# Causal mask of a second attention: added by VectorE in PSUM instead of by TensorE products, with one filling tile moved

## Chip, cores and metric

One core of one Trainium2 chip. The metric is the device time of one execution, in microseconds; three runs of the kernel before are given, and one more execution was profiled.

## The reference, cut to what matters

Two transformer blocks over 512 tokens of width 1024, in float32. The change lies in the attention of the second block, the "forgetting" attention with 16 heads of 64:

```python
def fox_attention(h, w_in, b_f, w_out):
    proj = h @ w_in                       # q, k, v of 16 heads, and 16 forget logits
    log_f = jax.nn.log_sigmoid(f_logit)
    c = lax.cumsum(log_f, axis=1).transpose(0, 2, 1)
    ...
        s = jnp.einsum('bhqd,bhkd->bhqk', qb, k, preferred_element_type=jnp.float32)
        s = s + cb[..., :, None] - c[..., None, :]
        s = jnp.where(k_pos[None, :] <= q_pos[:, None], s, NEG_INF)
        pr = jax.nn.softmax(s, axis=-1)
        return jnp.einsum('bhqk,bhkd->bhqd', pr.astype(v.dtype), v)
    ...
    return o @ w_out
```

All large products are computed in a split form: each operand is a high and a low part, and a product is three matmuls (high x high, high x low, low x high).

## The kernel before, in words

Every engine has its instructions in one order written out by hand, and semaphores tie them together. The weights come in "units" of 128 x 1024 (512 KB). SyncE loads a unit (L410), ScalarE makes its high part `w_hi` (L1856, helper `highs`), GpSimd its low part `w_lo` (L472), and TensorE multiplies it. Three buffers of each form a ring, so ScalarE's conversion of unit u + 3 waits until TensorE has finished unit u.

The second attention works in eight pairs of heads, p = 0 to 7. Its projections are 24 units, three per pair (q, k, v in that order). Eight "tiles" make up a unit; a tile is three matmuls of 128 x 512 (L519 to L521). Tiles are not done in a stage of their own: they fill the time in which the attention's chain would hold TensorE up. The list `FOX_FILL` (L179) says how many tiles stand behind each of the twelve places of a pair; `FOX_AHEAD` = 24 tiles are done before. The helper `fill` issues them, and `fox_made(p, i)` counts how many are done after place i. VectorE and ScalarE use the same count in `fox_evict`: when a unit is complete they scale it out of its bank (L1145), make its high part (L1845; q and k only) and its low part (L1622 or L1151), and ScalarE converts the weights of the unit three further on. For the last pair (p = 7) there are no tiles left and the first seven places hold steps of the output projection (`fill_out`).

TensorE's order in a pair (L1017 to L1030) is:

```python
scores(0); more(0)
scores(1); v_turn(); more(1)
scores(2); more(2)
scores(3); more(3)
turn(0, 0); turn(0, 1); more(4); pv(0, 0); turn(0, 2); more(5); pv(0, 1); turn(0, 3); more(6); pv(0, 2)
turn(1, 0); pv(0, 3); turn(1, 1); more(7)
pv(1, 0); turn(1, 2); more(8); pv(1, 1); turn(1, 3); more(9); pv(1, 2); more(10); pv(1, 3); more(11)
```

- `scores(qi)`, qi = 0 to 3, takes the query block qi of both heads against the first (qi + 1) * 128 keys, into PSUM banks 2 and 3. It waits until both exponentials of the step before are done (`A2["exps"]`). Four terms (L982) use 64 rows of the array for each head, the fourth adds the forget sums `c_head`; then one 128 x 128 product per head (L984), identity times the mask tile `causal_r` (0 on and below the diagonal, -1e30 above), adds the causal mask to the diagonal block and raises `A2["scores"]`.
- VectorE, `mx(qi)`: for each head `peak` (L1320 to L1322) waits for `A2["scores"]` and takes the negated row maximum. Between the steps stand `nrm(qi)` (reciprocal L1328, scaling L1331), the evictions, `out_low` and the low part of v, in this order: `mx(0)`, eviction and `out_low` of the pair before, `nrm(0)`, `mx(1)`, eviction, `nrm(1)`, `fv_lo`, `mx(2)`, eviction, `nrm(2)`, `mx(3)`, eviction, `nrm(3)`.
- ScalarE: two exponentials with row sums (L1992) per step, the high part of v (`fv_hi`), the next pair's `c_head` (L2260), and the conversions of the units.
- `turn(hd, kb)` transposes probabilities (L1000), ScalarE and VectorE split them into `fpt_hi` and `fpt_lo` (L1845, L1151), and `pv(hd, kb)` multiplies them with v (L1007 to L1009), waiting for `fpt_lo`.

Of the kernel before, what the change touches and what calls it, by code (L numbers as in the profile page):

```python
# [17 lines left out]
P = 128  # L18
# [23 lines left out]
F32 = mybir.dt.float32  # L42
F32R = mybir.dt.float32r
ALU = mybir.AluOpType
# [131 lines left out]


FOX_AHEAD = 24
FOX_FILL = [(2, 2, 3, 4, 2, 1, 1, 2, 1, 1, 1, 1)] * 6 + [(2, 2, 2, 3, 2, 1, 1, 1, 1, 1, 1, 1)]  # L179


def fox_made(p, i):

    return 3 * DC + FOX_AHEAD + sum(map(sum, FOX_FILL[:p])) + sum(FOX_FILL[p][:i + 1])

# [23 lines left out]
def build(nc, x_in, p_in, weights, vectors, last_gain, out):  # L209
# [4 lines left out]
    with ExitStack() as ctx:  # L214
# [7 lines left out]
        def sem(name):  # L222
            return ctx.enter_context(nc.semaphore(name))
# [17 lines left out]
        ident_r = sb("ident_r", [P, P], F32R)  # L241
        causal_r = sb("causal_r", [P, P], F32R)
# [95 lines left out]
        ps = ctx.enter_context(nc.psum_tensor("ps", [P, 8, S], F32))  # L338
# [23 lines left out]
        def stage_sems(stage, *names):  # L362
            return {n: sem(f"{stage}_{n}") for n in names}
# [8 lines left out]
        att_names = ("scores", "peak", "exps", "inv", "probs", "turned", "hi", "lo", "pv", "ohi", "olo")  # L372
        A1 = stage_sems("nsa", *att_names, "q", "qhi")
        s_cs = stage_sems("cmp_att", "scores", "sub", "exp", "stat", "probs")
        A2 = stage_sems("fox", *att_names, "qk", "qkhi", "vturned", "vhi", "vlo", "crow")
        s_fg = stage_sems("forget", "dve", "act")
        s_ffn = stage_sems("ffn", "tap", "conv", "t2", "gelu", "h", "hhi", "t")
        s_mlp = stage_sems("mlp", "t", "r", "s", "hi")
# [137 lines left out]
        def _(pe):  # L516
# [174 lines left out]
            for half in range(2):  # L691
                cols = slice(2 * P + half * P, 2 * P + (half + 1) * P)
                mm = three(ps[0:2 * NC1, 5, 0:P], hid_hi[:, 1, half, :], w_hi[:, uu % RING, cols], hid_lo[:, 1, half, :],
                           w_lo[:, uu % RING, cols], half == 0, half == 1)
# [45 lines left out]
            def fill(n):  # L740

                for at in range(made[0], made[0] + n):
                    part(u0 + at // DC, at % DC, at % DC + 1)
                made[0] += n
# [55 lines left out]
            for j in range(9):  # L800
                b = j - 1
# [31 lines left out]
            for tb in range(QB):  # L833
                mm = pe.matmul(ps[:, 3, tb:tb + 1], T[:, 1, tb * P:(tb + 1) * P], mean_ch[:, 0:1], start=True, stop=True)
# [3 lines left out]
            for tb in range(QB):  # L838
                mm = pe.matmul(ps[:, 3, tb * P:(tb + 1) * P], rms_c[:, 1, tb:tb + 1].to_broadcast([P, P]), ident[:], start=True, stop=True)
# [120 lines left out]
            def fox_here(k):  # L960
                pe.wait_ge(A2["olo"], CREDIT + 2 * k + 2)

# [6 lines left out]
            def fox_pair(p):  # L969

                par = p % 2
                q, k = (fq_hi[:, par, :], fq_lo[:, par, :]), (fk_hi[:, par, :], fk_lo[:, par, :])

                def scores(qi):

                    e, n = 8 * p + 2 * qi, (qi + 1) * P
                    pe.wait_ge(A2["exps"], e + 2)
                    qs = slice(qi * P, n)
                    for t, (a, b) in enumerate(((q[0][:, qs], k[0]), (q[0][:, qs], k[1]), (q[1][:, qs], k[0]), (ones_r, c_head))):
                        for hd in range(2):  # L980
                            rows = slice(hd * HD, (hd + 1) * HD)
                            pe.matmul(ps[:, 2 + hd, 0:n], a[rows, :], b[rows, 0:n], start=t == 0, stop=False)  # L982
                    for hd in range(2):
                        pe.matmul(ps[:, 2 + hd, qs], ident_r[:], causal_r[:], start=False, stop=True).then_inc(A2["scores"], 1)  # L984

                def v_turn():
                    pe.wait_ge(bank_free, u0 + 3 * p + 3)
                    pe.wait_ge(A2["lo"], CREDIT + 8 * p)
                    for tb in range(QB):
                        mm = pe.transpose(ps[:, 4, tb * P:(tb + 1) * P], fv[:, 0, tb * P:(tb + 1) * P], ident[:])  # L990
                    mm.then_inc(A2["vturned"], 1)

                def turn(hd, kb):
                    e = 8 * p + 4 * hd + kb
                    pe.wait_ge(A2["lo"], e + 1)
                    if kb == 0:
                        pe.wait_ge(A2["probs"], CREDIT + 8 * p + 7 + hd)
                    for qi in range(kb, QB):
                        off = P_OFF[qi] + kb * P
                        mm = pe.transpose(ps[:, 4 + kb % 2, qi * P:(qi + 1) * P], fprob[:, hd, off:off + P], ident[:])  # L1000
                    mm.then_inc(A2["turned"], 1)

                def pv(hd, kb):
                    pe.wait_ge(A2["lo"], 8 * p + 4 * hd + kb + 1 + CREDIT)
                    o = ps[:, 6 + hd, kb * P:S]
                    ph, pl = (t[:, kb % 2, kb * P:S] for t in (fpt_hi, fpt_lo))
                    pe.matmul(o, fv_hi[:, kb, :], ph, start=kb == 0, stop=False)  # L1007
                    pe.matmul(o, fv_hi[:, kb, :], pl, start=False, stop=False)
                    pe.matmul(o, fv_lo[:, kb, :], ph, start=False, stop=kb == QB - 1).then_inc(A2["pv"], 1)  # L1009

                def more(i):
                    if p < 7:
                        fill(FOX_FILL[p][i])
                    elif i < DC - 1:
                        fill_out(i)

                pe.wait_ge(bank_free, u0 + 3 * p + 2)  # L1017
                pe.wait_ge(A2["crow"], p + 1)
# [4 lines that stand above are left out]
                pe.wait_ge(A2["vlo"], p + 1)  # L1023
                pe.wait_ge(A2["olo"], p * 2 + 1)
                turn(0, 0); turn(0, 1); more(4); pv(0, 0); turn(0, 2); more(5); pv(0, 1); turn(0, 3); more(6); pv(0, 2)
                turn(1, 0); pv(0, 3); turn(1, 1); more(7)
                pe.wait_ge(A2["olo"], p * 2 + 2)
                if p == 0:
                    pe.wait_ge(bank_free, u0 + 6)
                pv(1, 0); turn(1, 2); more(8); pv(1, 1); turn(1, 3); more(9); pv(1, 2); more(10); pv(1, 3); more(11)  # L1030
# [75 lines left out]
            for h in range(2):  # L1106
                for j in range(4):
# [3 lines left out]
                    for kk, tb in (cells if h == 0 else sorted(cells, key=lambda c: c[1])):  # L1111
# [9 lines left out]
                        mm = three(ps[:, BANK[acc], :], xh, wh, xl, wl, k == 0, k == DC - 1)  # L1121
# [7 lines left out]
            for n in range(DC):  # L1129
# [5 lines left out]
                for m in range(4):  # L1135
                    mm = pe.transpose(ps[:, TURN_BANKS[n], m * P:(m + 1) * P], X[:, 4 * h + m, tb * P:(tb + 1) * P], ident[:])
# [4 lines left out]
        def _(dve):  # L1141
# [176 lines left out]
            scaled(U["gates"], T[:, 0:1, :])  # L1318

            def peak(A, e, par, st, qi, b):  # L1320
                dve.wait_ge(A["scores"], e + 1)
                dve.tensor_reduce(st[:, 0, par, qi:qi + 1], ps[:, b, 0:(qi + 1) * P], AX.X, ALU.max, negate=True).then_inc(A["peak"], 1)  # L1322

            def normalise(A, e, i, par, st, pr, qi, gate=None):
# [103 lines left out]
            for j in range(9):  # L1428
                p, br, b = j // 2, j % 2, j - 1
# [217 lines left out]
            for first in (32, 96):  # L1647
                rows = slice(first, first + 32)
# [18 lines left out]
            def fox_pair(p):  # L1667
                e0 = 8 * p

                def mx(qi):  # L1670
                    for hd in range(2):
                        peak(A2, e0 + 2 * qi + hd, hd, fstat, qi, 2 + hd)

                def nrm(qi):
                    for hd in range(2):
                        e = e0 + 2 * qi + hd
                        normalise(A2, e, e, hd, fstat, fprob[:, hd, :], qi)

                def lo(hd, kb):
                    split_turned(A2, e0 + 4 * hd + kb, kb % 2, (fpt_hi, fpt_lo), kb)  # L1680

                def out_low(p, hd):
                    rows = slice(hd * HD, (hd + 1) * HD)
                    dve.wait_ge(A2["ohi"], 2 * p + hd + 1)
                    low(fo_lo[rows, p:p + 1, :], ps[rows, 6 + hd:7 + hd, :], fo_hi[rows, p:p + 1, :], A2["olo"])

                def evict(i):
                    fox_evict(p, i)

                mx(0)  # L1690
                if p:
                    fox_evict(p - 1, 11)
                    out_low(p - 1, 1)
                nrm(0)
                mx(1); evict(0); nrm(1)
                dve.wait_ge(A2["vhi"], p + 1)
                low(fv_lo[:], ps[:, 4, :].rearrange("p (a b) -> p a b", b=P), fv_hi[:], A2["vlo"])
                mx(2); evict(1); nrm(2)
                mx(3); evict(2); nrm(3)
                evict(3)  # L1700
                lo(0, 0); lo(0, 1); evict(4); lo(0, 2); evict(5); lo(0, 3); evict(6); lo(1, 0); out_low(p, 0); lo(1, 1); evict(7)
                lo(1, 2); evict(8); lo(1, 3); evict(9); evict(10)
                if p == 7:
                    out_low(7, 1)
# [79 lines left out]
            for m in range(DC):  # L1784
                b, c, x = (bank(u0 + 3 * m + j) for j in range(3))
# [716 lines left out]
```

## Time and profile before

| what | us |
|---|---|
| three runs | 2181.45, 2186.0, 2184.88 |
| median | 2184.88 |
| the profiled execution, its own time | 2185.32 |
| span of its instructions | 2183.6 |

The profile is of one execution. PE is TensorE, DVE VectorE, ACT ScalarE, POOL GpSimd. A row of the timeline gives the start in us from the span's start, the length in us, the engine, the line, the operation, what is written and read, the shape, how often, and in brackets how long the engine was idle before and what ended that. A matmul's length is longer than its share of the engine, since matmuls overlap: the distance between two starts is what it costs.

### The profile page before, as it was taken

What the parts mean: (1) busy time and instruction counts of PE and PEld (TensorE: products, weight loads), DVE (VectorE), ACT (ScalarE), POOL (GpSimd) and SP (SyncE); (2) the same over time, 40 slices, a digit from 0 to 9 for tenths busy, and PEclk for the clock granted to TensorE, in tenths of its full rate; (3) what the DMA queues carried; (4) which work ended last, traced back from release to release, by engine and by line L of the source; (5) the groups of instructions that cost most, each with busy time, mean ns of one, the idle gap of its engine ahead of it and who ended that gap; (6) DMA issues with size and microseconds to landing.
All of it is one profiled execution on the core that took longest, in us unless ns stands there. A gap on an engine that the chain in (4) does not pass through costs nothing.

```text
span 2183.6 us, 25317 instructions
## 1 busy us (share of the span) xinstructions
PE 2148.8 (98%) x10198; PEld 1761.0 (81%) x10198; DVE 1009.0 (46%) x1630; ACT 873.0 (40%) x1365; POOL 933.5 (43%) x424
## 2 busy tenths in 40 slices
PE   9999999999999999999999999999999999999998
PEld 7877778888888887777778888888888888888886
DVE  5877775445524235556635422313643345122134
ACT  5434346444424254545434422324532244233234
POOL 5722124434444455322225444444554454444446
PEclk9999999999999999999999999999999999999999
DMA  4421112333333332211122333322323323333322
GB/s 159 148 74 43 45 49 82 91 97 106 97 97 97 97 116 78 70 57 49 49 68 87 96 97 97 97 96 87 97 87 97 97 85 98 97 97 97 96 80 85
DMA packets 53829, 193.27 MB, mean 89 GB/s; under 512 B 6096, under 2 KB 6224, under 8 KB 53712
## 3 DMA queue, kind: packets, MB, share of 16 engines
q1 hardware_dynamic: 52992, 189.81, 27.7%
q10 hardware_dynamic: 720, 1.84, 0.3%
q8 instruction: 81, 1.33, 0.2%
q14 instruction: 36, 0.29, 0.0%
HBM read 189.53 MB, written 2.10 MB: 88 GB/s over the span
## 4 chain that ended last, share of the span: by engine, by line
PE 90%; DVE 5%; ACT 4%; issue 1%; DMA 0%; POOL 0%; DVEq 0%; ACTq 0%; POOLq 0%
PE ps L519 27%; PE ps L521 27%; PE ps L520 27%; PE ps L982 1%; PE ps L733 1%; DVE ps L1211 1%; PE ps L713 1%; ACT w_hi L1856 1%; PE ps L725 1%; PE ps L1000 1%; PE ps L615 1%; ACT fprob L1992 1%; PE ps L1007 1%; PE ps L715 0%; DVE xg_lo L1171 0%
## 5 line engine op out<-in xcount | busy, mean ns | idle before, releaser
L472 POOL TENSOR_TENSOR w_lo<-w_raw,w_hi 128x1024 fp32r<-128x1024 f32 x352 | 852.0, 2422 | 1210.0 <-ACT w_hi L1856 1209.9
L519 PE MATMUL ps<-xg_hi,w_hi 128*128 128x512 f32 x1688 | 673.8, 399 | 5.0 <-POOL w_lo L486 2.6
L521 PE MATMUL ps<-xg_hi,w_lo 128*128 128x512 f32 x1688 | 660.9, 392 | 0.0
L520 PE MATMUL ps<-xg_lo,w_hi 128*128 128x512 f32 x1688 | 660.5, 391 | 0.0
L1856 ACT ACTIVATE w_hi<-w_raw 128x1024 fp32r<-128x1024 f32 x352 | 372.3, 1058 | 625.4 <-PE ps L521 622.6
L519 PEld LDWEIGHTS ps<-xg_hi,w_hi 128*128 128x128 f32 x1688 | 318.6, 189 | 68.5 <-issue 2.9
L521 PEld LDWEIGHTS ps<-xg_hi,w_lo 128*128 128x128 f32 x1688 | 318.4, 189 | 67.7
L520 PEld LDWEIGHTS ps<-xg_lo,w_hi 128*128 128x128 f32 x1688 | 319.1, 189 | 59.8
L521 PE MATMUL ps<-h_hi,w_lo 128*128 128x512 f32 x688 | 267.8, 389 | 0.0
L519 PE MATMUL ps<-h_hi,w_hi 128*128 128x512 f32 x688 | 267.7, 389 | 0.0
L520 PE MATMUL ps<-h_lo,w_hi 128*128 128x512 f32 x688 | 267.7, 389 | 0.0
L1145 DVE TENSOR_TENSOR ps<-ps,inv_rms 128x512 f32<-128x512 f32 x164 | 113.6, 695 | 194.2 <-PE ps L521 181.0
L519 PEld LDWEIGHTS ps<-h_hi,w_hi 128*128 128x128 f32 x688 | 129.2, 188 | 26.9
L520 PEld LDWEIGHTS ps<-h_lo,w_hi 128*128 128x128 f32 x688 | 129.2, 188 | 26.8
L521 PEld LDWEIGHTS ps<-h_hi,w_lo 128*128 128x128 f32 x688 | 129.2, 188 | 26.6
L1501 DVE TENSOR_TENSOR mixed<-mixed,ps 128x512 f32<-128x512 f32 x48 | 33.0, 688 | 199.9 <-PE ps L521 199.9
L1171 DVE SCALAR_TENSOR_TENSOR xg_lo<-resid,vec,xg_hi 128x512 fp32r<-128x512 f32 x72 | 87.0, 1212 | 12.3 <-ACT xg_hi L1882 10.1
L1211 DVE SCALAR_TENSOR_TENSOR ps<-glu,vec,ps 128x512 f32<-128x512 f32 x116 | 87.1, 751 | 1.9
L1845 ACT ACTIVATE h_hi<-ps 128x512 fp32r<-128x512 f32 x86 | 51.5, 598 | 90.1 <-DVE ps L1762 48.8
L481 POOL TENSOR_TENSOR sq_sum<-sq_sum,sq 128x512 f32<-128x512 f32 x42 | 66.5, 1583 | 25.2 <-ACT sq L1879 22.9
L1882 ACT ACTIVATE xg_hi<-resid,vec 128x512 fp32r<-128x512 f32 x72 | 51.7, 717 | 64.0 <-DVE resid L1501 40.2
L1762 DVE TENSOR_TENSOR ps<-tile_b,ps 128x512 f32<-128x512 f32 x64 | 44.6, 696 | 57.7 <-ACT tile_b L2300 57.7
(345 smaller groups left out, 2466.5 us busy)
## 6 DMA issues: line engine op xcount, KB each, us to landing
w_raw<-in_weights SPq DMA_DIRECT2D x352, 512.0 KB, 3.5
out_x<-mixed SPq DMA_DIRECT2D x8, 256.0 KB, 2.1
resid<-in_x SPq DMA_DIRECT2D x3, 512.0 KB, 7.2
p_raw<-in_p ACTq DMA_DIRECT2D x3, 512.0 KB, 3.6
resid<-in_x SPq DMA_DIRECT2D x2, 256.0 KB, 3.8
last_gain<-in_last_gain SPq DMA_DIRECT2D x1, 512.0 KB, 4.5
w_raw<-in_weights SPq DMA_DIRECT2D x1, 256.0 KB, 4.0
w_raw<-in_weights ACTq DMA_DIRECT2D x1, 256.0 KB, 4.2
```

The lines of the kernel that those rows point to most:

```text
L472: pool.tensor_tensor(w_lo[:, slot, :], w_raw[:, u % RAW, :], w_hi[:, slot, :].bitcast(F32), ALU.subtract).then_inc(w_ready, 1)
L481: pool.tensor_tensor(sq_sum[:], sq_sum[:], sq[:, m % 2:m % 2 + 1, :], ALU.add).then_inc(summed, 1)
L519: pe.matmul(o, w, x, start=start, stop=False)
L520: pe.matmul(o, w, xl, start=False, stop=False)
L521: return pe.matmul(o, wl, x, start=False, stop=stop)
L1145: dve.tensor_tensor(out, ps[:, BANK[u]:BANK[u] + 1, :], R[:], ALU.mult).then_inc(done, 1)
L1171: dve.scalar_tensor_tensor(xg_lo[:, m:m + 1, :], X[:, m:m + 1, :], g, xg_hi[:, m:m + 1, :].bitcast(F32), ALU.mult, ALU.subtract).then_inc( ...
L1211: ins = dve.scalar_tensor_tensor(acc if k < CONV_TAPS - 1 else conv_acc[:, ct, :], src, w, acc, ALU.mult, ALU.add)
L1762: dve.tensor_tensor(t, T2[:, m % 2:m % 2 + 1, :], t, ALU.mult).then_inc(s_mlp["s"], 1)
L1845: act.activation(out, x, ACT.Copy, scale=scale).then_inc(done, 1)
L1856: act.activation(w_hi[:, u % RING, :], w_raw[:, u % RAW, :], ACT.Copy).then_inc(w_hi_ready, 1)
L1882: act.activation(xg_hi[:, m:m + 1, :], X[:, m:m + 1, :], ACT.Copy, scale=g).then_inc(prep_hi, 1)
```

## The change

The mask products in `scores` go; the fourth score term now closes the sum, and the semaphore is raised once per step. On VectorE one add per step puts the mask on the diagonal blocks of both heads at once, in place in PSUM; a wait of VectorE on its own result follows, and then the two maxima, which no longer wait for TensorE themselves. In `FOX_FILL` one tile of each of the first six pairs moves from the eighth place (between `turn(1, 1)` and `pv(1, 0)`) to the second (behind `scores(1)` and `v_turn()`), and one of the seventh pair from the twelfth place to the second.

```diff
-FOX_FILL = [(2, 2, 3, 4, 2, 1, 1, 2, 1, 1, 1, 1)] * 6 + [(2, 2, 2, 3, 2, 1, 1, 1, 1, 1, 1, 1)]
+FOX_FILL = [(2, 3, 3, 4, 2, 1, 1, 1, 1, 1, 1, 1)] * 6 + [(2, 3, 2, 3, 2, 1, 1, 1, 1, 1, 1, 0)]
...
-        A2 = stage_sems("fox", *att_names, "qk", "qkhi", "vturned", "vhi", "vlo", "crow")
+        A2 = stage_sems("fox", *att_names, "masked", "qk", "qkhi", "vturned", "vhi", "vlo", "crow")
...
                         for hd in range(2):
                             rows = slice(hd * HD, (hd + 1) * HD)
-                            pe.matmul(ps[:, 2 + hd, 0:n], a[rows, :], b[rows, 0:n], start=t == 0, stop=False)
-                    for hd in range(2):
-                        pe.matmul(ps[:, 2 + hd, qs], ident_r[:], causal_r[:], start=False, stop=True).then_inc(A2["scores"], 1)
+                            mm = pe.matmul(ps[:, 2 + hd, 0:n], a[rows, :], b[rows, 0:n], start=t == 0, stop=t == 3)
+                    mm.then_inc(A2["scores"], 1)
...
             def peak(A, e, par, st, qi, b):
-                dve.wait_ge(A["scores"], e + 1)
                 dve.tensor_reduce(st[:, 0, par, qi:qi + 1], ps[:, b, 0:(qi + 1) * P], AX.X, ALU.max, negate=True).then_inc(A["peak"], 1)
...
                 def mx(qi):
+
+                    diagonal, step = ps[:, 2:4, qi * P:(qi + 1) * P], 4 * p + qi
+                    dve.wait_ge(A2["scores"], step + 1)
+                    dve.tensor_tensor(diagonal, diagonal, causal_r[:].bitcast(F32).unsqueeze(1).to_broadcast([P, 2, P]),
+                                      ALU.add).then_inc(A2["masked"], 1)
+                    dve.wait_ge(A2["masked"], step + 1)
                     for hd in range(2):
                         peak(A2, e0 + 2 * qi + hd, hd, fstat, qi, 2 + hd)
```

## Rows read from the trace of the kernel before

**Rows 1.** The page, busy time of each engine in the span.
```profile
PE 2148.8 (98%) x10198; PEld 1761.0 (81%) x10198; DVE 1009.0 (46%) x1630; ACT 873.0 (40%) x1365; POOL 933.5 (43%) x424
```
**Rows 2.** Busy time by stretches: us, each engine, clock, DMA share, GB/s.
```profile
170.00:180.00 10.00, 9.48 (x64) 7.64 (x63) 5.52 (x14) 3.67 (x10) 1.06 (x1) 0.83 0.08 34
900.60:1114.20 213.60, 205.24 (x1185) 160.68 (x1184) 127.11 (x311) 105.17 (x256) 46.69 (x20) 1.00 0.16 50
```
**Rows 3.** Timeline of TensorE, pair p = 2, 955 to 969 us.
```profile
955.21 0.33 PE L982 MATMUL ps<-fk_hi,fq_hi 64*128 64x128 f32 x2
...
955.60 0.27 PE L982 MATMUL ps<-c_head,ones_r 64*128 64x128 f32 x2
955.80 0.44 PE L984 MATMUL ps<-causal_r,ident_r 128*128 128x128 f32 x2
956.08 0.45 PE L519 MATMUL ps<-xg_hi,w_hi 128*128 128x512 f32 x1
...
957.59 0.39 PE L982 MATMUL ps<-fk_hi,fq_hi 64*128 64x256 f32 x2
...
960.49 0.45 PE L982 MATMUL ps<-fk_hi,fq_hi 64*128 64x384 f32 x2
...
963.87 0.50 PE L982 MATMUL ps<-fk_hi,fq_hi 64*128 64x512 f32 x2
...
967.39 0.39 PE L519 MATMUL ps<-xg_hi,w_hi 128*128 128x512 f32 x1
...
968.08 0.93 PE L1000 MATMUL ps<-ident,fprob 128*128 128x128 f32 x7
```
**Rows 4.** Timeline of VectorE, the same pair.
```profile
956.17 0.49 DVE L1322 TENSOR_REDUCE fstat<-ps 128x1 f32<-128x128 f32 x2 [0.66 <-PE ps L984]
...
958.00 0.16 DVE L1328 RECIPROCAL fstat<-fstat 128x1 f32<-128x1 f32 x1
958.20 0.29 DVE L1331 TENSOR_SCALAR fprob<-fprob,fstat 128x128 f32<-128x128 f32 x1
...
960.80 0.69 DVE L1151 TENSOR_TENSOR fv_lo<-ps,fv_hi 128x512 fp32r<-128x512 f32 x1
...
967.36 0.49 DVE L1331 TENSOR_SCALAR fprob<-fprob,fstat 128x512 f32<-128x512 f32 x1
```
**Rows 5.** Timeline of ScalarE, the same pair.
```profile
957.10 0.20 ACT L1992 ACTIVATION_READ_ACCUMULATOR fprob<-ps,fstat 128x1 f32 x1
...
959.90 0.20 ACT L1992 ACTIVATION_READ_ACCUMULATOR fprob<-ps,fstat 128x1 f32 x1
...
963.39 0.20 ACT L1992 ACTIVATION_READ_ACCUMULATOR fprob<-ps,fstat 128x1 f32 x1
...
968.05 1.05 ACT L1856 ACTIVATE w_hi<-w_raw 128x1024 fp32r<-128x1024 f32 x1
```
**Rows 6.** The mask products (ns min/median/max, first and last start); VectorE operations between PSUM and SBUF.
```profile
L984 PE MATMUL ps<-causal_r,ident_r x64: 272/302/329, 901.3 to 1098.2; 128*128 128x128 f32 x64
...
971.99 0.42 DVE L1151 TENSOR_TENSOR fpt_lo<-ps,fpt_hi 128x256 fp32r<-128x256 f32 x1 [1.22 <-ACT fpt_hi L1845]
972.34 0.69 DVE L1145 TENSOR_TENSOR ps<-ps,inv_rms 128x512 f32<-128x512 f32 x1
```
**Rows 7.** Timeline of TensorE (PEld: weight loads), pairs 2, 3, 6, 7; ScalarE, pair 3.
```profile
974.36 0.19 PEld L1007 LDWEIGHTS ps<-fpt_hi,fv_hi 128*128 128x128 f32 x1 [0.24 <-DVE fpt_lo L1151]
...
990.68 0.20 ACT L1992 ACTIVATION_READ_ACCUMULATOR fprob<-ps,fstat 128x1 f32 x1
...
990.93 0.50 PE L982 MATMUL ps<-fk_hi,fq_hi 64*128 64x512 f32 x2 [0.59 <-ACT fprob L1992]
...
1080.85 0.47 PE L519 MATMUL ps<-xg_hi,w_hi 128*128 128x512 f32 x1
...
1081.95 0.47 PE L1007 MATMUL ps<-fpt_hi,fv_hi 128*128 128x512 f32 x1 [0.17 <-DVE fpt_lo L1151]
...
1089.34 0.47 PE L519 MATMUL ps<-fo_hi,w_hi 128*128 128x512 f32 x1 [1.16 <-DVE fv L1145]
```

## Prediction, made before the result was known

> **What bounds the kernel now.** I read the page first. TensorE is busy 98% of the span, so whatever moves the time must move TensorE's own queue [rows 1]. The change touches only the second attention, so I read that stage next, by windows: 213.6 us, TensorE busy 205.2 of them, at a granted clock of 1.00 throughout [rows 2]. VectorE is busy 127 us there, so it has room on average; the question is whether it has room at the moment when TensorE waits for it. Eight head pairs take some 26.7 us each (213.6 / 8).
>
> Then the timeline of one pair, the third (p = 2), engine by engine [rows 3 to 5]. In its first half each of the four steps is a chain: scores on TensorE, two row maxima (L1322) on VectorE, two exponentials on ScalarE, and only then may the next scores start, since they use the same two PSUM banks. TensorE covers the chain with filling tiles. From one scores start to the next it takes 955.21 to 957.59 = 2.38 us, then 2.90, 3.38, and 4.21 to the first transposes at 968.08 [rows 3]. The exponentials end at 957.30, 960.10 and 963.59 (start plus 0.20 of the last row each) [rows 5], so TensorE comes 0.29, 0.39 and 0.28 after them. Where it really had to wait it started 0.05 after (990.93, its two exponentials done at 990.88) [rows 7]. The true cover is thus only 0.24, 0.34 and 0.23 us.
>
> **Part 1, the mask products go.** A pair of them takes 0.28 us of TensorE: 955.80 to the tile behind at 956.08 [rows 3]. There are 32 such pairs (L984 x64) [rows 6]. The change of array shape in front of them (955.60 to 955.80, 0.20) stays, now in front of the next tile. The tile behind may start its second product somewhat later than behind a mask, so I take 0.25 between 0.22 and 0.28: 8.0 us of TensorE work in all, if nothing waits.
>
> The Trainium skill ("TensorEngine Tiling (Array Packing)", Key Properties) says that a change of tiling mode drains TensorE; by that rule the 0.20 stays whole, as in the row; only if it went with the mask would up to 32 x 0.20 = 6 us more come off.
>
> **Part 2, the add on VectorE.** No row of before shows this add. The nearest is the same form from PSUM to SBUF, 128x256 in 0.42 us; at 128x512 an operation back into PSUM and one into SBUF take 0.69 each, so the destination costs nothing visible [rows 4, 6]. I take 0.43; the bounds are 0.29 (a 128x128 row) and 0.69 (the 128x512 rows) [rows 4, 6]. The maxima must wait for it: reciprocal to scaling, the same kind of wait, is 958.00 + 0.16 to 958.20, 0.04 us [rows 4]. In return the add starts earlier: the first mask product ends 0.30 after 955.80, the maximum follows at 956.17 (0.07 later); the last score product ends at 955.87, so the add can start at 955.94, 0.23 earlier [rows 3, 4, 6]. Each chain grows by 0.43 + 0.04 - 0.23 = **0.24 us**.
>
> **The sum for one pair**, step by step (TensorE arrives 0.25 earlier each time):
> - Step 0: wait 0.24 + 0.25 - 0.24 = 0.25. The gain of the mask is eaten: net 0.
> - Step 1: here VectorE itself is late. Its last scaling of step 0 ends at 958.49 [rows 4], now 0.24 later, 958.73, while the add could start at 958.40. The chain grows by 0.24 + 0.33 = 0.57. The moved tile comes here: 967.39 to 968.08, 0.69 [rows 3]. TensorE arrives 0.69 - 0.25 = 0.44 later against a cover of 0.34: no wait, 0.2 to spare. Net +0.44 (0.41 with a mask worth 0.28). Without the tile it would have waited.
> - Step 2: behind the second chain stand the scaling and fv_lo, 960.80 + 0.69 [rows 4], now 0.57 later: VectorE is free at 962.06 - 0.08 of overlap, where the add could start at 961.53 + 0.42. So the chain ends 0.80 later than before, the scores of step 3 start 0.57 later: net +0.16 on this step.
> - Step 3: the transposes wait for the first scaled rows, 967.36 + 0.49 = 967.85 [rows 4]; TensorE came at 968.08, and needs some 0.15. They start 0.57 + 0.24 - 0.08 = 0.73 later. In five of the pairs a conversion w_hi of 1.05 us [rows 5] stands on ScalarE between the exponentials and fpt_hi, and the whole chain (0.81) comes through at the first pv.
> - Second half: the tile is gone from behind turn(1, 1), -0.70. But pair 6 had one tile there all along, and it shows what then happens: from the tile at 1080.85 to pv(1, 0) at 1081.95 are 1.10 us where a tile takes 0.77 behind transposes; TensorE waited for fpt_lo [rows 7]. So 0.34 comes back, net -0.36.
>
> A plain pair is then 0.81 - 0.36 = **+0.45 us**, where a naive count says -1.0.
>
> **The unit boundaries** move too: seven of the 18 units that the tiles make up end one step earlier, each with a conversion of 1.05 us on ScalarE [rows 5], and for q and k a second one over half the columns, which I take as 0.6. POOL, which follows each conversion, and the loads on SP's queue come with them, but POOL is busy 47 of 214 us [rows 2] and TensorE waits for neither here. Where this matters:
> - p = 0: unit 7 now ends in front of hi(1, 0), which delays pv(1, 0) by the two conversions less the 0.6 that they start ahead: 0.62 - 0.70 + 1.03 = +0.95.
> - p = 2: unit 12 leaves the way of pv(0, 3), which had waited 0.24 [rows 7]: 0.45 - 0.25 = +0.20.
> - p = 3: the conversions already delay fv_hi, so that step 2 waited 0.59 [rows 7]; there is no cover. The delay of step 1 (0.60), an add that can't start early (0.47) and step 3 (0.24) all come through: 1.31 - 0.36 = +0.95.
> - p = 4: unit 17 now ends in front of hi(0, 0), where ScalarE had been free for the transposes: the 0.81 of the chain and 0.3 of the conversion, 1.10 - 0.36 = +0.74.
> - p = 5, step 1 already late on VectorE: +0.57. p = 1: +0.45.
> - p = 6: as p = 3 (1.31), and unit 22, a k with its second conversion, now stands in front of hi(0, 0): +1.04; the last tile is gone from its end: -0.70. Net +1.65.
> - p = 7 has no such tiles. The unit in front of it is now evicted in time, so the wait at 1089.34 (1.16 idle, 1.33 in all against an unhindered start) goes: step 0 falls from 3.75 to 2.38 (-1.37). The chain-bound rest costs 0.24 + 0.53 + 0.24 = +1.01. Net -0.36.
>
> Sum: 0.95 + 0.45 + 0.20 + 0.95 + 0.74 + 0.57 + 1.65 - 0.36 = **+5.15 us**. The profiled execution took 2185.32 us (span 2183.6 and 1.7 around it) and would take 2190.5. The median of the three runs is 2184.88, 0.4 less: forecast **2190.0 us**, +0.24%. A measurement of this kernel tells about 0.2%, 4.4 us, from no change.
>
> **Bounds of the unknown.** With an add of 0.29 each chain shrinks by 0.14, some three chains in eight pairs: -3.4 us, 2186.6. With 0.69 each grows by 0.26: +6.2, 2196. A plain pair's own error is about 0.3, times 8 is 2.4. The forecast case alone is 2187 to 2195.5.
>
> **Rivals.**
> 1. *Costs and gains cancel*, 2181 to 2189, likeliest 2185. The place is pv(1, 0): if fpt_lo comes in time behind one tile (in p = 2 by the timeline's account it nearly does), 7 x 0.34 = 2.4 us don't come back, and if the unit boundaries don't hurt, 2 to 3 more. Against it: the row of pair 6. Chance 0.35.
> 2. *TensorE stays the bound and the change is faster.* The place is the chain from scores to exponentials, the price 8.0 us of mask products and 1.3 of the wait in p = 7: 9.3, 2175.6. It decides where the chain's growth falls under 0.23 - 0.25, about zero: the add would have to start as the last score product ends and take under 0.2. Part of it (2176 to 2180) needs only shorter waits in steps 0 and 2. For it: TensorE 98% busy, stage waits of only some 8 us now. Against: cover of 0.24. Chance 0.17.
> 3. *The granted clock falls.* It was 1.00 in this stage, through the wait of 1.16 us too, but in 170 to 180 us, where the first attention's short products stand, it was 0.83 [rows 2]: 0.17 x 10 = 1.7 us lost each time. Twice makes 2193.5. Chance 0.06, inside the slower case.
>
> The Trainium skill ("TensorE: Matmul & The Clock Gate", The HAM clock gate) says that a less active TensorE is throttled to half rate, which speaks against trading its work for waits; the trace agrees at 170 us and not in this stage.
>
> 4. *The change isn't one in effect*: the add stands in each step's chain by its wait, and the tiles are counted (168 before and after), so I give this nothing.
>
> **Chances.** Slower by over 0.2% 0.48 (forecast 0.42, clock 0.06), within 0.2% 0.35, faster 0.17. The range of 8 in 10 reaches into rivals 1 and 2: 2179.5 to 2195.5.
>
> **What would show it.** L984 gone, 32 adds of 0.43 on VectorE, 0.04 before each maximum. Waits of TensorE for fprob in nearly every step 0 and 2 (4 before), at step 1 none in plain pairs; waits for fpt_lo of about 0.3 at most pv(1, 0); the wait at the start of p = 7 gone; the stage 213.6 + 5 = 219 us at clock 1.00. Wrong if the stage is shorter than 213 us, if scores of step 2 wait (then VectorE's delay is mis-sized), or if the time moved outside the stage.

## The result and the profile after

Nine timed runs of the changed kernel took 2186.00 to 2194.47 us, median **2189.73**; nine of the kernel before 2179.11 to 2186.21, median 2182.32. The ratio is 1.003 (95% interval 1.0018 to 1.0042): the change makes the kernel slower by 0.3%, 6.6 us between the means and 7.4 between the medians. The profiled execution took 2186.0 us, its span 2184.3.

The page of the changed kernel, busy time, against [rows 1]:

```profile
PE 2141.8 (98%) x10134; PEld 1748.4 (80%) x10134; DVE 1018.8 (47%) x1662; ACT 872.8 (40%) x1365; POOL 934.3 (43%) x424
```

TensorE has 64 products less and VectorE 32 instructions more, as the change says. The two profiled spans alone hide the loss (2184.3 against 2183.6), so I measured the **stage** in the timeline: from the first scores (L982) to the filling products behind the last pair. Before it is 900.72 to 1112.68, 211.96 us; after 897.69 to 1115.14, 217.44 us: **+5.48**. What lies outside the stage is 1971.6 before and 1966.9 after, though the change does nothing there; the two traces differ in the number of stretches at half the granted clock, all of them outside the stage (seven before, four after). The runs of one kernel scatter by 7 to 8.5 us too, so from here on the stage is what I compare.

Windows of the changed kernel (columns as in [rows 2]): the first half of the third pair, from its first scores to its first transposes, and the whole attention.

```profile
953.41:966.84 13.43, 12.95 (x73) 9.24 (x73) 11.06 (x31) 5.62 (x19) 1.53 (x1) 1.00 0.13 40
897.60:1115.20 217.60, 199.99 (x1116) 151.36 (x1116) 139.95 (x342) 103.39 (x254) 46.60 (x20) 1.00 0.15 49
```

And the same first half before:

```profile
955.21:968.08 12.87, 12.87 (x78) 9.69 (x78) 9.54 (x27) 5.72 (x20) 1.55 (x1) 1.00 0.13 42
```

There TensorE was busy all the time and VectorE 74% of it; now VectorE is busy 82% (11.06 of 13.43) and TensorE idles 0.48 us. Over the attention TensorE idles 17.6 us (217.60 less 199.99), where it idled 8.4 [rows 2]. The second of these windows and that of [rows 2] each reach slightly beyond the stage; cut to the stage the idle times are the same. The waits of TensorE in the attention (engine line waited for: total us, times, longest), first after, then before:

```profile
PE ps L982 <- ACT fprob L1996: 8.0, 10, 2.1
PE ps L1006 <- DVE fpt_lo L1150: 6.1, 14, 0.9
PE ps L999 <- DVE fprob L1329: 2.6, 6, 1.3
```

```profile
PE ps L982 <- ACT fprob L1992: 3.1, 4, 1.3
PE ps L1007 <- DVE fpt_lo L1151: 3.0, 6, 0.9
PE ps L519 <- DVE fv L1145: 1.2, 1, 1.2
PE ps L1000 <- DVE fprob L1331: 1.0, 2, 0.9
```

The scores wait for the exponentials 10 times, not 4, and the products with v for `fpt_lo` 14 times, not 6; only the one wait of 1.16 for an eviction [rows 7] is gone. These lists leave out waits under 0.15 us; in the timeline `scores(1)` and `scores(3)` now wait 0.10 or more in every pair, as the prediction said, and `scores(2)` in pairs 5 and 7 alone. TensorE did save its work. Every mask pair gone brought the next scores 0.22 us nearer (from the last term of the first scores, 953.79, to the second tile behind, 954.79, are 1.00 us; before, with the mask between, 955.60 to 956.82, 1.22). Here is the third pair's start, TensorE and then VectorE:

```profile
953.41 0.33 PE L982 MATMUL ps<-fk_hi,fq_hi 64*128 64x128 f32 x2
953.79 0.27 PE L982 MATMUL ps<-c_head,ones_r 64*128 64x128 f32 x2
954.00 0.50 PE L519 MATMUL ps<-xg_hi,w_hi 128*128 128x512 f32 x1
...
954.79 0.40 PE L519 MATMUL ps<-xg_hi,w_hi 128*128 128x512 f32 x1
...
955.76 0.39 PE L982 MATMUL ps<-fk_hi,fq_hi 64*128 64x256 f32 x2
...
959.09 0.44 PE L982 MATMUL ps<-fk_hi,fq_hi 64*128 64x384 f32 x2
...
962.51 0.50 PE L982 MATMUL ps<-fk_hi,fq_hi 64*128 64x512 f32 x2 [0.19 <-ACT fprob L1996]
...
966.84 0.96 PE L999 MATMUL ps<-ident,fprob 128*128 128x128 f32 x7 [0.19 <-DVE fprob L1329]
```

```profile
954.11 0.43 DVE L1672 TENSOR_TENSOR ps<-ps,causal_r 128x256 f32<-128x256 f32 x1 [0.42 <-PE ps L982]
954.58 0.49 DVE L1320 TENSOR_REDUCE fstat<-ps 128x1 f32<-128x128 f32 x2
...
956.61 0.29 DVE L1329 TENSOR_SCALAR fprob<-fprob,fstat 128x128 f32<-128x128 f32 x1
956.92 0.43 DVE L1672 TENSOR_TENSOR ps<-ps,causal_r 128x256 f32<-128x256 f32 x1
957.39 0.76 DVE L1320 TENSOR_REDUCE fstat<-ps 128x1 f32<-128x256 f32 x2
...
959.57 0.69 DVE L1150 TENSOR_TENSOR fv_lo<-ps,fv_hi 128x512 fp32r<-128x512 f32 x1
960.17 0.42 DVE L1672 TENSOR_TENSOR ps<-ps,causal_r 128x256 f32<-128x256 f32 x1
960.63 1.02 DVE L1320 TENSOR_REDUCE fstat<-ps 128x1 f32<-128x384 f32 x2
```

The add takes 0.43 us and the maxima begin 0.04 behind it (954.54 to 954.58). In step 1 the add starts when the scaling ends, not when the scores do: VectorE is late. From scores start to scores start it is 2.35, 3.33 and 3.42, then 4.33 to the transposes. From the last score term to the first product of the other shape it is still 0.21 (953.79 to 954.00), so that part of the mask's place stayed. Of these 0.21, about 0.11 are the term itself: that is the distance between two score terms of this width in both kernels (955.49 to 955.60 before). What the change of shape adds is about 0.1.

By the same reading, all eight pairs (us, from one pair's first scores to the next):

| pair | before | after | difference | forecast |
|---|---|---|---|---|
| 0 | 27.64 | 28.67 | +1.03 | +0.95 |
| 1 | 26.85 | 27.04 | +0.19 | +0.45 |
| 2 | 26.40 | 26.49 | +0.09 | +0.20 |
| 3 | 26.78 | 27.80 | +1.02 | +0.95 |
| 4 | 25.89 | 26.53 | +0.64 | +0.74 |
| 5 | 26.91 | 27.72 | +0.81 | +0.57 |
| 6 | 25.96 | 27.55 | +1.59 | +1.65 |
| 7 | 25.53 | 25.64 | +0.11 | -0.36 |
| sum | 211.96 | 217.44 | +5.48 | +5.15 |

### The profile page after: what moved, and what is told of

It reads as the page before. It is cut to its first block, busy times and chain, and to the rows that moved or that the text cites. A ratio compares the mean times of both kernels' runs of the same rounds, so it can differ in the third digit from the quotient of the medians.

```text
span 2184.3 us, 25221 instructions
## 1 busy us (share of the span) xinstructions
PE 2141.8 (98%) x10134; PEld 1748.4 (80%) x10134; DVE 1018.8 (47%) x1662; ACT 872.8 (40%) x1365; POOL 934.3 (43%) x424
## 3 DMA queue, kind: packets, MB, share of 16 engines
q8 instruction: 80, 1.31, 0.2%
## 4 chain that ended last, share of the span: by engine, by line
PE 86%; DVE 8%; ACT 5%; issue 1%; DMA 0%; POOL 0%; DVEq 0%; ACTq 0%; POOLq 0%
PE ps L519 26%; PE ps L521 26%; PE ps L520 26%; ACT fprob L1996 1%; PE ps L733 1%; DVE ps L1210 1%; ACT w_hi L1860 1%; PE ps L713 1%; DVE fstat L1320 1%; PE ps L982 1%; PE ps L725 1%; PE ps L1006 1%; DVE ps L1672 1%; PE ps L615 1%; DVE xg_lo L1170 1%
```

## Experiments

In each, the time is that of a profiled execution, with one execution of the kernel before on the same chip where no more are named. A single time settles little, since the runs of one kernel differ by 7 us; what is compared is the "stage", the length defined above, from one trace of each.

**1. The add alone, tiles where they were.** From the changed kernel:

```diff
-FOX_FILL = [(2, 3, 3, 4, 2, 1, 1, 1, 1, 1, 1, 1)] * 6 + [(2, 3, 2, 3, 2, 1, 1, 1, 1, 1, 1, 0)]
+FOX_FILL = [(2, 2, 3, 4, 2, 1, 1, 2, 1, 1, 1, 1)] * 6 + [(2, 2, 2, 3, 2, 1, 1, 1, 1, 1, 1, 1)]
```

> The add on VectorE in place of the mask products, with the tiles where they stood before. The attention stage, from its first scores to the filling products behind it, is 212.0 us before and 217.5 after. Theory (the chain through VectorE sets the steps, and the moved tile only covers the step where VectorE is late): step 1 becomes chain-bound, 3.13 us against 2.89, some 0.5 us more per pair up to the first pv, the second half of a pair as before, and the wait at the start of pair 7 stays; stage 216.5 to 218.5. Rival (TensorE is the bound and the tile move is what costs): stage 204 to 206. Rival (only the moved tile costs, the add is neutral): 212.

Measured: 2191.34 us (before 2181.97), stage 219.21, 0.7 above the range. In a plain pair the two middle steps are 3.16 and 3.58. About 0.8 us of the stage is a stretch at half clock that begins about 1.5 us behind a long wait in the seventh pair (the last step there takes 4.86, in pair 3 it takes 4.08). The start of the scores, and windows before and from there on:

```profile
1072.92 0.50 PE L982 MATMUL ps<-fk_hi,fq_hi 64*128 64x512 f32 x2 [2.28 <-ACT fprob L1996]
```

```profile
1068.00:1074.00 6.00, 3.64 (x22) 2.37 (x22) 4.59 (x12) 3.18 (x8) 2.38 (x1) 1.00 0.25 63
1074.00:1078.00 4.00, 4.00 (x13) 3.03 (x12) 3.02 (x7) 2.06 (x5) 0.00 (x0) 0.57 0.09 37
```

The granted clock was 1.00 while TensorE idled (busy 3.64 of 6.00) and 0.57 after it, mostly at the lower of its two levels, 1.2 GHz. The changed kernel has a wait of 2.14 at the same place and kept its clock. Without that stretch the stage is some 218.4, inside the range and 6.4 above before: the add alone costs more than the whole change, and the moved tile gives back 1.0.

**2. The moved tiles alone.** The kernel before, masks on TensorE, with the new `FOX_FILL`.

> The moved tiles alone, mask products on TensorE as before. Theory: no wait needs the tile at step 1, so step 1 grows by 0.69 and the second half of a pair gives back only 0.36, because fpt_lo comes late behind one tile; the wait at the start of pair 7 (1.3) goes and the waits of 0.6 at step 2 of pairs 3 and 6 are covered: stage 212.5 to 214.5. Rival (moved work is only moved): 210.5 to 211, the 1.3 us of pair 7 less than before.

Measured: 2186.01 us (before 2181.97), stage 213.55, +1.6: as expected. Here too the products with v wait 14 times for `fpt_lo`, 5.6 us, against 7 times in experiment 1: the new waits come from the moved tiles, not from the add. Six of the eight new ones stand at `pv(1, 0)`, behind the place that the tile left (0.17 each, 0.81 in the first pair).

**3. No mask at all.** From the kernel before: the score products are the last of their banks, and neither engine adds a mask, so this kernel leaves the causal mask out altogether.

```diff
-                            pe.matmul(ps[:, 2 + hd, 0:n], a[rows, :], b[rows, 0:n], start=t == 0, stop=False)
-                    for hd in range(2):
-                        pe.matmul(ps[:, 2 + hd, qs], ident_r[:], causal_r[:], start=False, stop=True).then_inc(A2["scores"], 1)
+                            mm = pe.matmul(ps[:, 2 + hd, 0:n], a[rows, :], b[rows, 0:n], start=t == 0, stop=t == 3)
+                    mm.then_inc(A2["scores"], 1)
```

> Leaves the causal mask of the second attention out (neither products nor add), tiles as before. The price of the mask products by themselves. Theory: TensorE's work and the chain both shrink by 0.22 per step, 32 x 0.22 = 7 us: stage 204 to 206.5. Rival (the products were hidden in waits): 210 to 212.

Measured: 2179.22 us (before 2181.97), stage 205.71. The mask products are worth 6.3 us when nothing takes their place, 0.20 a step, so the saving that the change aims at exists. From here to the add alone (218.4) is 12.7 us, 0.40 per add, of the 0.47 that an add and its wait take.

**4. The add twice.** The second adds the mask once more.

```diff
-                    dve.tensor_tensor(diagonal, diagonal, causal_r[:].bitcast(F32).unsqueeze(1).to_broadcast([P, 2, P]),
-                                      ALU.add).then_inc(A2["masked"], 1)
-                    dve.wait_ge(A2["masked"], step + 1)
+                    for again in range(2):
+                        dve.tensor_tensor(diagonal, diagonal, causal_r[:].bitcast(F32).unsqueeze(1).to_broadcast([P, 2, P]),
+                                          ALU.add).then_inc(A2["masked"], 1)
+                        dve.wait_ge(A2["masked"], 2 * step + again + 1)
```

> The changed kernel with the mask added twice, each add with its wait (masked scores are twice as negative, nothing else changes). Theory: every chain grows by another 0.47, all of it seen in steps 0, 2 and 3 and 0.28 of it in step 1, where the moved tile has 0.2 to spare: 1.7 us per pair, stage 217.5 + 13.5 = 231 (229 to 233). Rival (VectorE is off TensorE's path, it is 64% busy): 217.5 to 219.

Measured: 2201.22 us (before 2181.97), stage 231.48: 14.04 us for 32 more adds, 0.44 each. About 0.3 us of it is a stretch at half clock in the seventh pair (1086 to 1089 us), which leaves 0.43 each. Nearly the whole duration of an add reaches the end. TensorE, busy 98% of the span, does not bound the attention in this kernel; the chain does.

**5. The high part of v ahead of an eviction on ScalarE**, on the changed kernel. In pairs 3 and 6 step 2 takes 4.68 us because `fv_hi` waits behind a unit's conversions:

```profile
985.26 1.05 ACT L1860 ACTIVATE w_hi<-w_raw 128x1024 fp32r<-128x1024 f32 x1
986.21 0.59 ACT L1849 ACTIVATE fk_hi<-ps 128x512 fp32r<-128x512 f32 x1
986.69 0.60 ACT L1849 ACTIVATE fv_hi<-ps 128x512 fp32r<-128x512 f32 x1
...
987.33 0.69 DVE L1150 TENSOR_TENSOR fv_lo<-ps,fv_hi 128x512 fp32r<-128x512 f32 x1 [0.97 <-ACT fv_hi L1849]
987.93 0.42 DVE L1672 TENSOR_TENSOR ps<-ps,causal_r 128x256 f32<-128x256 f32 x1
```

In ScalarE's order `ex(0); ex(1); evict(0)`, `fv_hi`, `ex(2)` became `ex(0); ex(1)`, `fv_hi`, `evict(0); ex(2)`.

> The changed kernel, but ScalarE makes v's high part before it converts the units that end at place 0. Theory: in pairs 3 and 6 step 2 takes 4.68 us instead of 3.43 because fv_lo, and behind it on VectorE the add of step 2, wait for these conversions; both fall to 3.43, so the stage goes from 217.4 to 215.0 (214.3 to 215.6). Rival (the conversions delay ex(2) just as much where they stand now): 217 to 217.8.

Measured: stage 215.24, 2.2 us shorter, step 2 of both pairs 3.61. (Its one time is 2190.89; 17 of the kernel before on the same chip lie between 2178.39 and 2186.45.) Two pairs of eight lost what a queue on ScalarE put between v and the add.

**6. VectorE's order turned round: the maximum first.** On experiment 1:

```diff
-                nrm(0)
-                mx(1); evict(0); nrm(1)
+                mx(1); nrm(0); evict(0); nrm(1)
+                mx(2)
...
-                mx(2); evict(1); nrm(2)
+                evict(1); nrm(2)
```

> The add with the tiles of before (as e1, stage 219.2 with a stretch of half clock in it), but VectorE takes the maxima of step 1 before it scales the rows of step 0, and makes fv_lo behind the maxima of step 2. Theory (it is VectorE's own queue that is late in steps 1 and 2, by 0.33 and 0.15 and by 1.4 in pairs 3 and 6): step 1 falls from 3.16 to 2.83, step 2 to 3.42 in all pairs, stage 211 to 213.5, which is the kernel before. Rival (the add itself costs it, wherever it stands): 217 to 219.

Measured: 2196.49 us (17 of the kernel before: 2178.39 to 2186.45), stage **226.07: a miss by 13 us, in the wrong direction**. Step 1 fell from 3.16 to 2.78, as expected, but step 2 grew to 3.77, since `nrm(0)` and `nrm(1)` now both stood in front of `mx(2)`; and in pairs 1 and 4 step 3 took 6.33 and 6.58. There one scaling took 2.42 us where the same line takes 0.42; in pairs 3 and 6 the same happened to a scaling of step 1, and step 2 took 5.91 and 5.90. Both lines of VectorE, and GpSimd's beside them:

```profile
935.37 0.42 DVE L1329 TENSOR_SCALAR fprob<-fprob,fstat 128x384 f32<-128x384 f32 x1
...
936.09 2.42 DVE L1329 TENSOR_SCALAR fprob<-fprob,fstat 128x384 f32<-128x384 f32 x1
```

```profile
935.90 2.39 POOL L472 TENSOR_TENSOR w_lo<-w_raw,w_hi 128x1024 fp32r<-128x1024 f32 x1 [11.95 <-ACT w_hi L1860]
```

Four scalings were held so (2.42, 2.10, 2.42, 2.08), each until 0.2 us behind the end of the GpSimd instruction (938.51 against 938.29 here). Their steps are longer than in the plain pairs by 2.0, 2.1, 2.3 and 2.1, 8.5 in all; two stretches at half clock (0.57 in 941 to 945 and in 1077 to 1085 us) cost about 2 more.

**7. The high part of v first and one tile moved, on the kernel before:** `fv_hi` first as in 5, and the last tile of pair 6 from its last place to its third.

```diff
-FOX_FILL = [(2, 2, 3, 4, 2, 1, 1, 2, 1, 1, 1, 1)] * 6 + [(2, 2, 2, 3, 2, 1, 1, 1, 1, 1, 1, 1)]
+FOX_FILL = [(2, 2, 3, 4, 2, 1, 1, 2, 1, 1, 1, 1)] * 6 + [(2, 2, 3, 3, 2, 1, 1, 1, 1, 1, 1, 0)]
```

> The kernel before, with mask products on TensorE, and two edits: v's high part ahead of the conversions on ScalarE, and the last tile of pair 6 moved to its step 2, so that unit 23 is out of its bank when pair 7 starts. Theory: step 2 of pairs 3 and 6 falls from 4.05 to 3.39 (1.3 us), the wait of 1.35 at the start of pair 7 goes and the tile fills a wait: stage 209 (208.3 to 209.8), whole kernel 3 us (0.13%) faster than before.

Measured: stage 209.98, 2.0 below before and 0.2 above the range: unit 22 now ended in front of the transposes of pair 6, whose first product with v waited 0.82, which the expectation had left out. Median 2180.76 (12 runs) against 2181.79 (17 runs), ratio 0.9997 (0.9988 to 1.0006): not to be told from no change.

**8. The orders of 6 with those of 7:** the add on VectorE, VectorE's order of 6, ScalarE's order and the tiles of 7.

> The add on VectorE, with the order of VectorE as in e6, v's high part first as in e5 and the tiles as in e8. Theory: the chain is still what sets steps 0, 2 and 3, so the 7 us of mask products stay unearned: stage 209.5 to 211.5, whole kernel 1 to 2 us faster than before and 5 to 7 faster than the changed one, but not faster than e8. Rival (once VectorE's queue is in order, TensorE is the bound and the products' 7 us come off): 204 to 206.

Measured: 2196.22 us (6 runs), ratio 1.0067 (1.0055 to 1.0079), stage 223.93. The same miss as in 6, and again four scalings of 2.42 us each beside GpSimd. (This expectation was written before 6 had run.)

**9. GpSimd's instruction cut in half**, to test that reading. On 6, `w_lo` is made as two instructions of 512 columns for the units of this attention.

```diff
+                if not U["fox"] <= u < U["fox_out"] + 8:
+                    ...
+                pool.tensor_tensor(w_lo[:, slot, 0:UW // 2], w_raw[:, u % RAW, 0:UW // 2], w_hi[:, slot, 0:UW // 2].bitcast(F32),
+                                   ALU.subtract)
+                pool.tensor_tensor(w_lo[:, slot, UW // 2:UW], w_raw[:, u % RAW, UW // 2:UW], w_hi[:, slot, UW // 2:UW].bitcast(F32),
```

> As e6 (stage 226.1), but GpSimd makes w_lo of the units of this attention in two instructions of 512 columns. In e6 four scalings of VectorE (SBUF to SBUF) took 2.08 to 2.42 us instead of 0.35 or 0.42, each until the GpSimd instruction that ran beside it had ended. Theory (such a scaling waits for the end of the running GpSimd instruction): with instructions half as long these four take 1.0 to 1.3, stage 221 to 222.5. Rival (the long scalings have another cause, such as a late semaphore or the data): 2.1 to 2.4 again, stage 225.5 to 226.5.

Measured: 2189.80 us (10 of the kernel before: 2182.22 to 2187.69), stage 221.68, 4.4 below experiment 6. The four scalings took 1.31, 1.00, 1.31 and 1.00, together 4.4 less. Both stages hold stretches at half clock (two in 6, three here); step by step, what else differs between the two comes to nearly nothing. The first of these scalings and the instruction beside it:

```profile
935.42 1.29 POOL L476 TENSOR_TENSOR w_lo<-w_raw,w_hi 128x512 fp32r<-128x512 f32 x1 [11.80 <-ACT w_hi L1866]
...
935.62 1.31 DVE L1335 TENSOR_SCALAR fprob<-fprob,fstat 128x384 f32<-128x384 f32 x1
```

The scaling ends 0.22 behind the GpSimd instruction in both, so the hold is GpSimd's, and its length follows GpSimd's instruction.

**10. One more conversion out of the way, on 7.** In ScalarE's second half:

```diff
-                evict(2); evict(3)
-                hi(0, 0); hi(0, 1); evict(4); hi(0, 2); evict(5); hi(0, 3); evict(6); hi(1, 0); out_hi(0); hi(1, 1); evict(7)
+                evict(2)
+                hi(0, 0); hi(0, 1); evict(3); evict(4); hi(0, 2); evict(5); hi(0, 3); evict(6); hi(1, 0); out_hi(0); hi(1, 1); evict(7)
```

> As e8, and ScalarE makes fpt_hi of the first two transposes before it converts the unit that ends at place 3 (it is the q of pair 2 or 3 in pairs 0 and 1, a v in pair 3). Theory: the waits of 0.65, 0.86 and 0.13 for fpt_lo at the first pv of pairs 0, 1 and 3 go, pair 5 keeps its own, since its unit ends at place 2: stage 210.0 - 1.6 = 208.4 (208 to 209), whole kernel 3.5 us faster than the kernel before. Rival (the conversion is then late for a later wait): 209.5 to 210.5.

Measured: stage **206.98**, 1.0 below the range (the wait of 0.82 that 7 had made went too). Median 2178.26 (6 runs) against 2184.98 (10 runs), ratio 0.9968 (0.9956 to 0.9980): **faster than the kernel before**, by 0.3%, with the masks on TensorE. (Against the changed kernel there is only the stage, 10.5 shorter; the two were not timed side by side.) In the second pair, ScalarE and the first product with v, in the kernel before and then in this one:

```profile
941.43 1.06 ACT L1856 ACTIVATE w_hi<-w_raw 128x1024 fp32r<-128x1024 f32 x1
942.87 0.97 ACT L1845 ACTIVATE fpt_hi<-ps 128x512 fp32r<-128x512 f32 x2
944.24 0.50 PE L1007 MATMUL ps<-fpt_hi,fv_hi 128*128 128x512 f32 x1 [0.69 <-DVE fpt_lo L1151]
```

```profile
941.85 0.98 ACT L1845 ACTIVATE fpt_hi<-ps 128x512 fp32r<-128x512 f32 x2 [0.56 <-PE ps L1000]
942.72 1.07 ACT L1856 ACTIVATE w_hi<-w_raw 128x1024 fp32r<-128x1024 f32 x1
943.37 0.39 PE L1007 MATMUL ps<-fpt_hi,fv_hi 128*128 128x512 f32 x1
```

**11. The same two orders of ScalarE on the changed kernel.**

> The changed kernel with both reorderings of ScalarE, those of e5 and of e10. Theory: they take the waits of 0.96, 0.44, 0.18 and 0.96 for fpt_lo at the first pv of pairs 1, 3, 4 and 6 away (pairs 0 and 5 keep theirs, their units end at place 2): stage 215.2 - 2.5 = 212.7 (212 to 213.5), still 5 to 6.5 above the 207.0 of e10, which has the mask products on TensorE: the price of the add is in VectorE's part of the chain and not in how the units fall. Rival (the change costs only through where units end): 207 to 209.

Measured: 2184.81 us (before 2182.45), stage 212.31: 5.1 below the changed kernel, and still 5.3 above experiment 10. Clearing ScalarE's queue helps both forms of the mask alike (5.1 here, 5.0 from before to 10); it does not pay for the change. Experiments 10 and 12 differ in the tiles' places as well as in the mask, so the 5.3 is not the add's price alone. Up to the first transposes the eight pairs here are 5.5 longer in all, behind them 0.1 shorter.

## Why the prediction was right, point by point

The forecast was 2190.0 us and slower; the median is 2189.73, and the stage grew by 5.48 where 5.15 was summed. That the two times meet within 0.3 us is luck: the forecast added 5.1 to a median of 2184.88 from three runs, the nine runs of the same kernel, those three among them, have 2182.32, and the growth measured against those is 6.6 to 7.4. The mechanism stands in experiments 1, 3 and 4: masks worth 6.3 us, the add 12.7, and 0.44 of every further add at the end. No rival's case came: costs and gains did not cancel, TensorE did not stay the bound, and the clock stayed at 1.00 in the attention of the changed trace. The third rival was not far: experiments 1, 4, 6, 8 and 9 had eight stretches at half clock in the attention.

- **Part 1, a mask pair worth 0.25 to TensorE:** it was 0.22, the lower bound.
- **The array's change of shape stays whole:** 0.21, against 0.20 before. (The prediction took all of the 0.20 for the change of shape; 0.11 of it is the score term itself, so had it gone, some 3 us would have come off and not 6.) The rule of the Trainium skill that the prediction weighed here ("TensorEngine Tiling (Array Packing)", Key Properties) agrees with the trace.
- **Part 2, the add 0.43, its wait 0.04:** exact on both.
- **Step 0 nothing:** 2.36 against 2.38. **Step 1 +0.44:** +0.43, no wait of TensorE before the scores of step 2, VectorE late by its own scaling.
- **Step 2 +0.16:** too high; it was +0.04. The step that failed is a sum, not a view: the prediction has VectorE free at 962.06 less 0.08, an add of 0.43 and a wait of 0.04, which puts the maximum at 962.45, 0.69 behind its old start at 961.76; it wrote 0.80. With 0.69 the step comes out at +0.05. In the trace the add starts at 960.17, 6.76 behind the pair's first scores, and those numbers say 6.77.
- **Step 3, transposes +0.73 late in all:** 0.62 with the slip put right, and +0.56 measured in pair 2 (13.43 against 12.87). The forecast treated the pairs alike, and they are not: in pair 2 an eviction stands in front of the last scalings, and TensorE waits 0.19 for them; in pair 1 it had gone by before, the scaled rows are there at 939.40, TensorE comes at 939.54, and the step is 0.14 shorter. Pair 1 and then pair 2, VectorE:

```profile
938.71 0.16 DVE L1326 RECIPROCAL fstat<-fstat 128x1 f32<-128x1 f32 x1 [0.25 <-ACT fprob L1996]
938.91 0.49 DVE L1329 TENSOR_SCALAR fprob<-fprob,fstat 128x512 f32<-128x512 f32 x1
...
965.42 0.68 DVE L1144 TENSOR_TENSOR fv<-ps,inv_rms 128x512 f32<-128x512 f32 x1
966.02 0.15 DVE L1326 RECIPROCAL fstat<-fstat 128x1 f32<-128x1 f32 x1
966.21 0.49 DVE L1329 TENSOR_SCALAR fprob<-fprob,fstat 128x512 f32<-128x512 f32 x1
```

- **Second half, only 0.36 given back:** right in kind. Experiment 2 shows the new waits for `fpt_lo`, 14 instead of 6, without any add; at `pv(1, 0)` they are 0.17. In pair 2 the half gave back 0.47, in pair 1 0.12.
- **Unit boundaries, pairs 0, 3, 4, 6:** within 0.1 of the measured differences. That pairs 3 and 6 lose a full microsecond to `fv_hi` behind the conversions is shown by experiment 5, which took 1.07 off each. In pair 3 the agreement is partly luck: up to its transposes it lost 0.92 where the prediction has 1.31 less 0.08, and the half behind them gave back nothing (+0.10) where it has -0.36.
- **Pair 5, +0.57:** too low, +0.81. Step 1 alone grew by 0.72. VectorE was late there before too, with `fq_lo` and `fo_lo` in front of the scaling, and took the maxima of step 1 the moment it was free (3.90 behind the pair's first scores). Now it is free 0.22 later, and the add and its wait of 0.47 stand in front: 0.69 of the 0.72.
- **Pair 7, -0.36:** the largest miss, +0.11. The wait at its start went, step 0 fell to 2.39 as forecast. But step 1 grew by 0.79, not 0.53. A scaling took 0.83 (0.29 where nothing holds it), while GpSimd's instruction ran beside it to 1092.86. It had been held before the change as well (0.70), but there VectorE idled 0.49 before the next maxima, which hid it; now the add starts as soon as the scalings are done. In experiment 2 the same scaling took 0.98 and step 1 grew by 0.30 without any add. Step 2 grew by 0.45, not 0.24. First after, then before:

```profile
1090.46 2.40 POOL L472 TENSOR_TENSOR w_lo<-w_raw,w_hi 128x1024 fp32r<-128x1024 f32 x1 [10.25 <-ACT w_hi L1860]
...
1092.12 0.83 DVE L1329 TENSOR_SCALAR fprob<-fprob,fstat 128x128 f32<-128x128 f32 x1
...
1093.57 0.43 DVE L1672 TENSOR_TENSOR ps<-ps,causal_r 128x256 f32<-128x256 f32 x1
```

```profile
1090.15 0.70 DVE L1331 TENSOR_SCALAR fprob<-fprob,fstat 128x128 f32<-128x128 f32 x1
...
1091.93 0.76 DVE L1322 TENSOR_REDUCE fstat<-ps 128x1 f32<-128x256 f32 x2 [0.49 <-PE ps L984]
```

The slip in step 2 made the forecast about 0.1 too high in each of the plain pairs, some half a microsecond in all. The total came out well partly because errors of both signs met: 0.47 low in pair 7 and 0.24 in pair 5, some 0.5 high in pairs 1, 2, 4 and 6. Where the prediction was careless is GpSimd: it dismissed it as busy 47 of 214 us, and asked only whether TensorE waits for it, not whether VectorE does.

One sum looks open and nearly closes. Idle time grew by 9.2 us (17.6 less 8.4), so TensorE's busy time in the stage fell by only 3.8, though without any mask (experiment 3) it falls by 7.3. A product's row is 0.39 long while the next one starts 0.23 behind it, so in front of each wait some 0.16 of a row's tail counts as busy. The changed kernel has 25 waits more than the one before (39 against 14, short ones counted). By this estimate that is 4.0 us, against the 3.5 that are missing.

One thing stays open: why the clock falls behind some waits and not behind others. The length of the wait does not tell. It kept 1.00 behind 2.14 us in the changed kernel and behind 3.03 in pair 3 of experiment 8 (1.00 in 992 to 996 us), and it fell behind 2.28 in experiment 1 and behind 1.57 in pair 3 of experiment 9 (0.51 in 992.2 to 995.6).

## What to carry to other kernels

An engine that is 98% busy may still not set the time of a stage: look at how many tenths of a microsecond it arrives behind its chain, and take work off it only where the chain has more cover than the work's new place adds to it. Two changes of order on a half-idle engine (a conversion behind instead of in front of the value that the chain wants) were worth 5 us here, about what the whole change lost. Before VectorE's instructions are shifted, look at what GpSimd runs at the place that they are shifted to.

## What was unexpected in the hardware

- **VectorE's scaling is held until a GpSimd instruction ends.** From SBUF to SBUF, 128x384 in float32, 0.42 us alone took 2.42 beside a GpSimd subtraction of 2.39, and 1.31 beside one of 1.29. It happens in the kernel before too, twice in the attention (0.54 and 0.70 for the 0.29 of 128x128). In the attention of all 13 traces no scaling lies wholly inside a GpSimd instruction: each that started beside one ended behind it. VectorE's instructions that read PSUM lie inside by the hundred and keep their times (the add 0.42 to 0.43), and so does the reciprocal of one column (0.15 to 0.17). The Trainium skill ("SBUF — State Buffer", SBUF: two separate sides) says that VectorE, in some of its modes, and GpSimd share a port pair, which whichever starts first holds for its whole instruction while the other blocks; the traces agree, with these numbers.
- **The granted clock can fall after one wait, but need not**: it was 0.57 in 1074 to 1078 us, behind a wait of 2.28, in experiment 1. In all there are eight such stretches in the attention of five traces (experiments 1, 4, 6, 8 and 9), and none in those of the kernel before and the changed one. The Trainium skill ("TensorE: Matmul & The Clock Gate", The HAM clock gate) has the rule that the prediction weighed, that a less active TensorE is set to half rate; these five traces agree in kind.
